# Splitting a 256-token Fourier product by token parity, with the small matmuls around it put in another order, in a kernel of three transformer blocks on one core

## The reference, cut to what matters

```
def bidir_long_conv(u, h, skip):                       # twice, on 512 channels
    U = jnp.fft.rfft(u.astype(jnp.float32), n=2 * L, axis=1)
    Kf = jnp.fft.rfft(k, n=2 * L, axis=0)
    y = jnp.fft.irfft(U * Kf[None], n=2 * L, axis=1)[:, :L]
    return (y + u * skip)

z = parts[0]                                           # hyena_branch
for o in range(2):
    z = parts[o + 1] * bidir_long_conv(z, filt[:, o], skip[o])

h2 = h * rsqrt(mean(h * h) + eps) * norm_g * sigmoid(o)  # mlstm_branch, 4 heads of 128, 2 directions
y = (g_a * (y_a @ w_branch_hy) + g_b * (y_b @ w_branch_ml)) @ w_out

aff = softmax(h @ w_router)                            # 256 x 1024 @ 1024 x 16
gate, idx = lax.top_k(aff.T, 32)                       # each of 16 experts takes 32 tokens
ye = (silu(xg @ w1) * (xg @ w3)) @ w2                  # 24 MB of weights per expert
```

## Time and profile before

| | |
|---|---|
| median of 3 executions | 2276.26 us (2274.9 to 2278.98) |
| the profiled execution's own time | 2276.84 us |
| its span (first to last instruction) | 2275.1 us |
| TensorE busy | 1914.0 us, 84% |
| VectorE busy | 1036.5 us, 46% |
| ScalarE busy | 654.0 us, 29% |
| moved by DMA | 659.76 MB, mean 290 GB/s |
| chain that ended last | TensorE 57%, DMA 32%, VectorE 7%, ScalarE 3% |

### The profile page before, as it was taken

One profiled execution on the slowest core, in us unless ns is written; L12 is line 12 of the kernel. 1 busy time (PEld: TensorE's weight loads), 2 busy tenths in 40 slices (PEclk: granted clock), 3 DMA queues, 4 the chain that ended last, 5 costly groups with the idle time before them and its releaser, 6 DMA issues.

```text
span 2275.1 us, 26884 instructions
## 1 busy us (share of the span) xinstructions
PE 1914.0 (84%) x11476; PEld 1313.4 (58%) x11476; DVE 1036.5 (46%) x1340; ACT 654.0 (29%) x741; POOL 9.5 (0%) x6
## 2 busy tenths in 40 slices
PE   7999997665666665665577999999999999999998
PEld 4888782111111111111122888898888888898887
DVE  6777562000000000000011777567767777567776
ACT  4444240000000000000001444564444434564433
POOL 1000000000000000000000000000000000000000
PEclk9999998888877788788888999999999999999999
DMA  9362689999999999999999545444544555434442
GB/s 397 132 259 79 262 354 404 431 429 431 433 433 433 431 431 430 433 433 433 429 431 425 216 189 194 177 154 180 195 190 185 204 195 197 173 144 185 186 185 102
DMA packets 36253, 659.76 MB, mean 290 GB/s; under 512 B 4024, under 2 KB 4536, under 8 KB 6976
## 3 DMA queue, kind: packets, MB, share of 16 engines
q1 hardware_dynamic: 34144, 650.56, 69.5%
q10 hardware_dynamic: 2016, 7.84, 0.9%
HBM read 657.34 MB, written 1.05 MB: 289 GB/s over the span
## 4 chain that ended last, share of the span: by engine, by line
PE 57%; DMA 32%; DVE 7%; ACT 3%; issue 1%; SPq 0%; ACTq 0%; DVEq 0%
PE ps L1673 56%; DMA ring_b<-experts_dram 20%; DMA ring<-experts_dram 9%; DMA ring<-stream_dram 2%; PE ps L1682 1%; DVE ring_lo L1401 1%; ACT att_area L891 1%; DVE area_n L1441 0%; ACT area_n L791 0%; DVE mixer_area L1571 0%; DVE att_area L1567 0%; DVE ring_lo L1070 0%; DVE expert_area L1388 0%; DVE x_tok L1452 0%; ACT w_hi L750 0%
## 5 line engine op out<-in xcount | busy, mean ns | idle before, releaser
L1401 DVE TENSOR_TENSOR ring_lo<-ring,w_hi 128x2048 fp32r<-128x2048 f32 x168 | 384.7, 2291 | 195.9 <-ACT w_hi L750 195.9
L1673 PE MATMUL ps<-u_both,w_hi 128*128 128x512 f32 (+1 forms) x1792 | 398.0, 360 | 0.0
L750 ACT CAST w_hi<-ring 128x2048 fp32r<-128x2048 f32 x168 | 321.1, 1911 | 228.0 <-PE ps L1673 190.9
L1673 PEld LDWEIGHTS ps<-u_both,w_hi 128*128 128x128 f32 x1792 | 317.5, 189 | 48.5 <-issue 0.7
L726 ACT ACTIVATE expert_area<-ps 128x512 f32<-128x512 f32 x16 | 9.6, 597 | 836.3 <-PE ps L1673 836.3
L1673 PE MATMUL ps<-u_both,ring_lo 128*128 128x256 f32 x1536 | 238.4, 283 | 0.0
L1673 PE MATMUL ps<-ring_b,area_h 128*32 128x512 f32 x976 | 150.1, 770 | 89.2 <-DMA ring_b<-experts_dram 80.9
L1673 PE MATMUL ps<-ring,area_h 128*32 128x512 f32 x1024 | 149.8, 739 | 86.1 <-DMA ring<-experts_dram 78.3
L1372 DVE TENSOR_TENSOR expert_area<-expert_area,ps 128x512 f32<-128x512 f32 x16 | 11.0, 688 | 461.3 <-PE ps L1673 461.3
L1673 PEld LDWEIGHTS ps<-u_both,ring_lo 128*128 128x128 f32 x1536 | 213.2, 191 | 6.2
L1673 PEld LDWEIGHTS ps<-ring_b,area_h 128*32 128x32 f32 x976 | 35.3, 136 | 198.9 <-DMA ring_b<-experts_dram 102.0
(11 more groups left out here) (418 smaller groups left out, 2315.1 us busy)
## 6 DMA issues: line engine op xcount, KB each, us to landing
ring<-stream_dram SPq DMA_DIRECT2D x114, 2048.0 KB, 7.5
ring_b<-experts_dram SPq DMA_DIRECT2D x45, 4096.0 KB, 31.2
ring<-experts_dram SPq DMA_DIRECT2D x45, 4096.0 KB, 31.2
ring<-experts_dram SPq DMA_DIRECT2D x5, 2048.0 KB, 16.8
ring_b<-experts_dram SPq DMA_DIRECT2D x6, 1024.0 KB, 9.4
area_n<-norm_rows_dram ACTq DMA_DIRECT2D x6, 512.0 KB, 5.4
x_tok<-x_dram SPq DMA_DIRECT2D x2, 1024.0 KB, 8.0
spare<-experts_dram SPq DMA_DIRECT2D x1, 2048.0 KB, 17.9
```

The lines of the kernel that those rows point to most:

```text
L750: A.copy(upper_part(n), ring[:, n % RING, :]).then_inc(sig("alone_hi_ready") if n in ALONE else sig("w_hi_ready"), 1)
L1401: V.tensor_tensor(ring_lo[:, n % RING, :], ring[:, n % RING, :], upper_part(n).bitcast(F32), ALU.subtract).then_inc(sig("alone_ready") if ...
L1673: ins = M.matmul(out, lhsT, rhs, start=start, stop=stop, **more)
```

## The change

- **Parity.** Even and odd tokens are turned apart (a step of two in `hy(...)[:, t::2]`). With half as many frequencies per product, `dft` takes 4 matmuls in place of 8: the odd tokens' into banks 2 and 3, the even tokens' into banks 0 and 1. ScalarE copies the odd ones out (`odd_z`); VectorE makes sum and difference (`signal_halves`, 4 instructions per order). After the filter's product it makes the four sums and differences that `idft` now takes (4 more), and `idft` is 16 matmuls of 128 tokens in place of 256. z is then written with a step of two.
- **Units.** Units 33 to 36 and the first two `ada` steps of row 2 lie in order 0, ahead of `idft`; unit 37 at the start of order 1, unit 38 in halves. Banks, and what waits for what, go along with it. `lower_first(21)` lies behind `signal_halves(1)`.
- **Splits.** `lower_first(13)` lies behind the first head step, and 14, 15 and 16 each a step later; 16 behind the first head's `pairs_ready`. `ada_row(1, 4)` lies behind the first `kw_ready`. TensorE waits for the last state copy (`inter_kept`) only ahead of the state products.
- **Router.** `wrouter` is the stationary operand: 8 matmuls of 128 tokens per half, in four column quarters that add up side by side in PSUM; VectorE copies them out (`parts`), and one matmul with a 0/1 matrix (`fold`) adds the quarters. SyncE's wait at L456 goes along.

```diff
-                if o >= 1:
-                    act.wait_ge(sig("signal_ps"), ORDERS + o)
+                    act.wait_ge(sig("signal_ps"), ORDERS + 2 * o)
                 A.copy(z_tok, ps[:, 4:6, :]).then_inc(sig("z_kept"), 1)
                 if o == 0:
                     merge_gates(31, of=ACT.Identity)
+                act.wait_ge(sig("signal_ps"), ORDERS + 2 * o + 1)
+                A.copy(odd_z, ps[:, 2:4, :]).then_inc(sig("hT_odd"), 1)
...
                     merge_gates(32, 33)
                     upper_first(20)
-                    merge_gates(34, 35)
+                    merge_gates(34, 35, 36, 37)
                 else:
-                    merge_gates(36)
                     upper_first(21)
-                    merge_gates(37, 38, 39, 40)
+                    merge_gates(38, 39, 40)
...
-                lower_first(6 + i)
+                if i < 7:
+                    lower_first(6 + i)
...
-            ada_row(1, 4)
...
+                if h == 0:
+                    ada_row(1, 4)
                 if h == 2:
                     ada_col(1, 4)
-                if h > 0:
+                if h < 3:
                     lower_first(13 + h)
...
-                if h >= 2:
-                    lower_first(15 + h)
+                if h != 1:
+                    lower_first((16, None, 17, 18)[h])
...
+            def signal_halves(o):
+
+                dve.wait_ge(sig("hT_odd"), ORDERS + o + 1)
+                dve.wait_ge(sig("signal_ps"), ORDERS + 2 * o + 2)
+                for i in range(2):
+                    V.tensor_tensor(yspec[:, i, 0, :], bank(i), odd_z[:, i, :], ALU.add)
+                    last = V.tensor_tensor(yspec[:, i, 1, :], bank(i), odd_z[:, i, :], ALU.subtract)
+                step(last)
+
+            signal_halves(0)
...
+                if o == 1:
+                    signal_halves(o)
+                    lower_first(21)
...
+                for i in range(2):
+                    V.tensor_tensor(yt[:, 2 * i, :], yspec[:, i, 0, :], yspec[:, i, 1, :], ALU.add)
+                    last = V.tensor_tensor(yt[:, 2 * i + 1, :], yspec[:, i, 0, :], yspec[:, i, 1, :], ALU.subtract)
                 last.then_inc(sig("yspec_ready"), 1)
...
-                    step(V.scalar_tensor_tensor(z, z, col("skip", 4 * o + j),
-                                                bank(4 + j // 2)[:, (j % 2) * T:(j % 2 + 1) * T], ALU.mult, ALU.add))
+                    by_parity = z.rearrange("p (m e) -> p e m", e=2)
+                    y = bank(4 + j // 2)[:, (j % 2) * T:(j % 2 + 1) * T].rearrange("p (e m) -> p e m", e=2)
+                    step(V.scalar_tensor_tensor(by_parity, by_parity, col("skip", 4 * o + j), y, ALU.mult, ALU.add))
...
+            for t in range(TT):
+                dve.wait_ge(sig("logits_ps"), t + 1)
+                V.tensor_copy(parts[:, t, :], bank(4 + 2 * t)[:, 0:P]).then_inc(sig("logits_ready"), 1)
...
-            pe.wait_ge(sig("inter_kept"), H)
...
-                        turn(bank(4 + t)[:, j * P:(j + 1) * P], hy(4 * o + j)[:, t * P:(t + 1) * P],
+                        turn(bank(4 + t)[:, j * P:(j + 1) * P], hy(4 * o + j)[:, t::2],
...
-                for j in range(2):
-                    for k in range(TT):
-                        for t in range(TT):
-                            mm(bank(2 * j + k), dft[:, j, t, k * P:(k + 1) * P], z_tok[:, t, :],
+                for e in (1, 0):
+                    for j in range(2):
+                        mm(bank(2 * e + j), dft[:, j, e, :], z_tok[:, e, :], ready=sig("signal_ps") if j == 1 else None)
...
+                for r in range(2):
+                    for g in range(4):
+                        k = 2 * r + g // 2 + 4 * (g % 2)
+                        mm(bank(4 + 2 * t)[32 * g:32 * g + 32, 0:P], wrouter[:, k * NE:k * NE + 32],
+                           h2T[:, k, t * P:(t + 1) * P], start=r == 0, stop=r == 1,
...
```

More of the change, by code:

```diff
@@ L261, in build @@
         r = Region(tables, 0, N_TABS)
-        dft = r.take(2, TT, T)
-        idft = r.take(2, TT, T)
+        dft = r.take(2, 2, P)
+        idft = r.take(2, 2, P)
         causal = r.take(2, 384)
@@ L1940, in _ @@
                 else:
[L1941 to L1943 removed]
+                    merge_steps((38, 0, 4))
                 pe.wait_ge(sig("z_kept"), o + 1)
@@ L2045, in _, with logit_parts @@
             turn_half(0)
-            def logits(t):
-                for k in range(KD):
-                    if k % 4 == 0:
-                        pe.wait_ge(sig("h2T_ready") if k == 0 else sig("h2T_ready_v"), t + 1)
-                    mm(bank(4 + 2 * t)[:, 0:NE], h2T[:, k, t * P:(t + 1) * P], wrouter[:, k, :],
-                       start=k == 0, stop=k == KD - 1, ready=sig("logits_ps") if t == 1 and k == KD - 1 else None)
+            def logit_parts(t):
+                pe.wait_ge(sig("h2T_ready"), t + 1)
+                pe.wait_ge(sig("h2T_ready_v"), t + 1)
+                for r in range(2):
[3 more added lines that the diff above has]
+                           h2T[:, k, t * P:(t + 1) * P], start=r == 0, stop=r == 1,
+                           ready=sig("logits_ps") if r == 1 and g == 3 else None)
+            def logits(t):
+                pe.wait_ge(sig("logits_ready"), t + 1)
+                mm(bank(4 + 2 * t)[:, P:P + NE], parts[:, t, :], fold,
+                   ready=sig("logits_ps") if t == 1 else None)
             pe.wait_ge(sig("biases_loaded"), 32)
@@ L2066, in _ @@
             turn_half(1)
-            logits(0)
-            logits(1)
+            for t in range(TT):
+                logit_parts(t)
+            for t in range(TT):
+                logits(t)
             stream_in(0, 1)
@@ L2611, in lay_out @@
     out["vbias"] = np.tile(b_in[ML + 1024:ML + 1536][None, :], (P, 1))
-    out["wrouter"] = a["w_router"][0].reshape(KD, P, NE).transpose(1, 0, 2)
+    fold = np.zeros((P, NE), np.float32)
+    for g in range(4):
+        fold[32 * g + np.arange(NE), np.arange(NE)] = 1.0
+    out["wrouter"] = np.concatenate([a["w_router"][0].reshape(KD, P, NE).transpose(1, 0, 2).reshape(P, KD * NE),
+                                     np.zeros((P, NE), np.float32), fold], axis=1)
     out["fin_rows"] = np.stack([np.tile(a["final_norm_g"][None, :], (P, 1)), np.tile(a["final_norm_2"][None, :], (P, 1))])
```

79 lines of the change are left out of this document (36 added, 43 removed).

## The result

The changed kernel takes **2264.21 us** (median of 5 runs, 2261.92 to 2265.4) against 2275.22 for the kernel before beside it: ratio 0.9948, 95% interval 0.9933 to 0.9962. That is faster, 2.0 us above the forecast of 2262.2 and inside its range. The profiled execution has a span of 2263.5 us, 11.6 less than before's.

A forecast was written before the change was run, and what follows sets the result against it. Bound: the experts' weight stream, by its start and idle time. 12.0 us before its start plus 2.0 from the router give 14.0 off the profiled 2276.84: 2262.8; the median stands 0.6 lower, so 2262.2 us, range 2259.0 to 2267.0.

The forecast's parts named there:

- The heads: Recurrent heads: TensorE's waits of 1.66, 0.56 and 0.87 us go; 3.1 us gained, kept ends 2.2 and 3.5.
- Order 0: Convolution's first order: `dft` 3.55 us, `idft` 3.8; the second `dft` product starts at 243.9, where it was 247.81.
- rival 2: Convolution: halving the columns gains nothing in `idft`, which takes 6.8 us as before; 2265.2 us, chance 0.09.
- The one guess: VectorE's writing of z: reading and writing with a step of two adds 0.8 us.
- rival 1: Convolution's z and turning: the step of two costs twice on both engines; 2264.2 us, chance 0.12.
- Order 1: Convolution's second order: slot 39 is used at 249.75 instead of 261.76, so the train of transfers starts 12.0 us earlier.
- no bound: Convolution's weight slots 38 to 43 don't limit the path, since their pairs are asked for 8 to 15 us sooner.
- The branch: Branch products behind the second order: start at 276.4 instead of 288.4; the transfer of pair 48/49 decides by about 1 us.
- Router: Router logits ahead of the experts' refill: done at 336.9, 2.0 us less, bounds 1.0 and 2.9.
- Rival 3: Router: its gain goes to nothing, since partial sums, copy and fold hand over three times; 2264.2 us, chance 0.08.
- Rival 6: Order 0: TensorE waits through ScalarE if pair 38/39 lands later than about 231; 2279 us at 30 us, chance 0.04.
- Small things at no cost: Table load, router weights and SyncE's wait: `wrouter` grows by 32 words but no instruction waits for it; no cost.

The follow-up runs named there:

- e7_no_heads: The changed kernel with the recurrent heads' splits, the row and the wait for `inter_kept` back where they were; 2268.42 us.
- e11_ada_late: The changed kernel with the two moved `ada` steps put back into the second order, behind the turning of z; 2270.84 us.
- e10_x_late: The changed kernel with the reload of x issued behind the pair of slots 48/49 instead of ahead of it; 2262.96 us.
- e8_no_router: The changed kernel with the router's logits as before: tokens' columns as stationary operand, no partial sums; 2265.86 us.
- e1_before_pad32: The kernel before with an unused tensor of 32 words a partition behind the router's weights, so everything later lies 128 bytes higher; 2278.16 us, ratio 1.0012.
- e2_after_laid: The changed kernel with `topi` laid over the router weights' added columns, so later tensors lie as in the kernel before; 2260.91 us, ratio 0.9931.
- e9_laid_ring_b32: The changed kernel with `topi` laid over the router weights and `ring_b` (with `tabs2` and what is behind it) 128 bytes higher; 2259.15 us, ratio 0.9927.
- e13_best: As e9_laid_ring_b32, with x reloaded behind pair 48/49 and `cols` allocated ahead of `ring`, which moves `ring` to byte 1280; 2261.99 us.

## Why the prediction was right, and where it was not

Event by event, in us. "Forecast" is the prediction's working, "shown" the two profiled executions.

| step | forecast | shown |
|---|---|---|
| start of the heads (other execution) | 0 | -1.2 |
| heads (to the first `dft` product) | 3.1 | 3.5 |
| first to second `dft` product | 0.8 | 1.7 |
| second `dft` product to pair 44/45 | 8.1 | 7.8 |
| pair 44/45 to the experts' first weights | 0 | 1.1 |
| from there to the refill | 2.0 | 2.2 |
| experts' loads | 0 | 1.8 |
| layers, and the 57.4 us ahead of them | 0 | -5.4 |
| sum (of the unrounded values) | 14.0 | 11.6 |

- **The heads.** All three waits went, as forecast, and no split was late. The term was 0.4 too small by the table and 0.7 by `e7_no_heads`; the table's 3.5 has 0.3 in it that were lost ahead of the first head. The extra lies at the same three places. Ahead of the rows that started at 160.73, 174.85 and 182.86 (160.38, 173.66 and 180.59 now), TensorE gained 1.8, 0.8 and 1.1 us where its waits had been 1.66, 0.56 and 0.87. The rows right behind a wait had taken 1.16, 1.10 and 1.61 us and take 1.05, 1.03 and 1.50.
- **Order 0.** `dft` 3.67 against 3.55, `idft` 3.59 from its start to the next group (233.83 to 237.42) against 3.8, VectorE's work done at 233.6 against 232.9. The same 32 rows of `idft` at half the columns take 0.53 of the time, down to 128: rival 2 is out. The one guess, 0.8 us for the step of two, was nothing (0.48 and 0.48), and rival 1 is out with it. Of the Trainium skill's two rules the trace agrees with the note on cachelines in the page SBUF — State Buffer (float32 may step by up to four). The 1.7 to 2.5 ns per column of the page Vector Engine (DVE) Microarchitecture Reference, Measured stream behaviour on trn2, do not show as a cost of the step: 0.48 us for 256 columns is 1.9 ns with and without it. So no run tells what the step would cost an instruction that is faster per column.
- **Order 1.** The numbers held: slot 39 used at 249.8, pair 48/49 landed at 271.37 (forecast 272.2). The path was wrong. The prediction has "the landing follows the moment at which TensorE has used slot 39", and slots 38 to 43 as "no bound". Their loading is none in the changed kernel (ScalarE splits slot 42 at 246.58 without a wait), but the use of slots 42 and 43 is what releases pair 48/49. In `e11_ada_late` pair 44/45 went out 1.6 us later and pair 48/49 landed 6.7 later, at 278.05, with the queues idle from 264 to 266 us (DMA share 0.00). The chain of the kernel before already goes through pair 42/43, VectorE's split of slot 42 and the products with it:

```profile
247.94 11.54 DMA ring<-stream_dram
...
263.87 7.05 PE ps L1673 x56
```

and in the changed kernel through the same split, now at 249.98, which no longer waits for its weights but for VectorE's own sums and differences ahead of it:

```profile
252.32 7.08 PE ps L1693 x56
...
259.80 11.57 DMA ring<-stream_dram
```

Pair 48/49 was issued 11.5 us earlier by this path and pair 44/45 went out 11.9 earlier by the other; that the two agree within 0.4 us is luck. The two moved `ada` steps carry 6.5 of the 9.5 us of both orders (`e11_ada_late`), through the release of pair 42/43. No run undoes the parity split itself, so what it gives alone wasn't measured.
- **The branch.** "The transfer decides, by about 1 us" held: `e10_x_late` gave 1.0.
- **Router.** 2.0 forecast (its events, 339.04 and 336.9, give 2.1), 1.5 by `e8_no_router` and 2.2 by the traces. The gain against before has the clock in it, which the working left out: the row of 5.63 us had been taken while the clock fell. Rival 3 is out.
- **Rival 6.** Pair 38/39, issued at 219.80, was there at 227.7 and not at 231. The queue's issues before and after it were at 196.26 and 233.05, so it was alone, and 8 us were enough.
- **What failed** is the sentence under "Small things at no cost": "`wrouter` is 32 words wider, no instruction waits for it". Nothing waits for it, and it cost 5.2 us in the layers and gave back some 2 to 3 in the experts' loads, net 2.5 (`e1_before_pad32`) to 3.4 (`e2_after_laid`). The forecast started from 2276.26, and the kernel before took 2275.22 beside the changed one, so the gain was 11.0 us and not 14.0. The median still came within 2 us of the forecast because the steps ahead of the refill gave about 2.3 more than forecast (0.4 + 0.9 - 0.3 + 1.1 + 0.2 in the table) and this took it again: the right sum, partly by two errors of opposite sign, which is luck.

## What to carry to other kernels

A tensor that grows moves every tensor that is allocated behind it; compare the same long stretch of untouched work in both traces (here 851 rows, 161.1 and 162.1 us) before you look for a reason in the edit. Lay new scratch over something dead, or pad on purpose, and measure two or three places: here the best and the worst were 14 us apart (2259.15 and 2272.79), more than the whole change gave. And read what a moved step is worth from every buffer that it releases, not only from the one whose transfer is next on the chain.

## What the runs showed of the hardware

- Most groups of matmuls of 128x512 float32 rows took 389 to 390 ns or some 5 ns more by where tensors lie modulo 256 bytes. `w_hi` with `hid_lo` took 389 in `e9_laid_ring_b32` and 395 in `e13_best`, with neither of the two moved. The layers took 1005.8, 1008.6, 1011 or 1016.7 us with the same instructions and a granted clock of 1.00.
- The experts' stream of loads, half of which go into `ring_b`, ran 0.2 to 0.4% faster where it begins on a multiple of 256 bytes (855.0 to 856.5 us in ten profiled executions, 858.0 to 858.8 in the four others; `e9_laid_ring_b32` moves it without the layers' tensors). Moving `ring` onto such a multiple gained nothing (856.3).
- A step of two float32 words, in and out, costs this VectorE instruction nothing at 256 columns: 0.48 us with and without. TensorE's eight transposes of the operand read with that step took 1.12 us in order 0 and 1.23 in order 1 (behind a wait), against 1.04 and 1.03 without.
- TensorE's granted clock fell to 0.50 within the router's 32 rows of 16 columns and was at 1.00 all through the 36 rows that took their place. In `e11_ada_late` it fell to 0.50 behind 4 us in which TensorE stood still, and was 1.00 again from 262 us on.
